# V pages asked for by ScalarE in place of GpSimd, and VectorE's order rearranged, in a decoder layer

## The reference, cut to what matters

```
q, k, v, b, c, xv = split(rmsnorm(x) @ w_in)            # 1024 -> 3072
attn = stick-breaking attention, 8 heads of 64
conv = b * causal_conv3(c * xv)
h = x + concat(rmsnorm(attn), rmsnorm(conv)) @ w_out
h = h + cross_attention(rmsnorm(h), memory K/V)          # 4 heads, 256 memory tokens
h = h + swiglu(rmsnorm(h))
y = rmsnorm(h)
```

## Time and profile before

| | us |
|---|---|
| median of 3 runs | 1208.37 (1198.38 to 1223.24) |
| profiled execution | 1211.09, span 1209.3 |
| PE busy | 1072.4 (89%) |
| VectorE busy | 665.9 (55%) |
| ScalarE busy | 321.4 (27%) |
| GpSimd busy | 409.9 (34%) |

### The profile page before, as it was taken

One profiled execution on the slowest core, in us unless ns is written; L12 is line 12 of the kernel. 1 busy time (PEld: TensorE's weight loads), 2 busy tenths in 40 slices (PEclk: granted clock), 3 DMA queues, 4 the chain that ended last, 5 costly groups with the idle time before them and its releaser, 6 DMA issues.

```text
span 1209.3 us, 28991 instructions
## 1 busy us (share of the span) xinstructions
PE 1072.4 (89%) x11527; PEld 917.1 (76%) x11527; DVE 665.9 (55%) x909; ACT 321.4 (27%) x486; POOL 409.9 (34%) x341
## 2 busy tenths in 40 slices
PE   6889999996678867888599888899999999999997
PEld 3677887774445445556499858899999999999996
DVE  2745647677477676654379356755553002554544
ACT  3412121231233523333422153411211112112121
POOL 0524544442232233444332103343433333433330
PEclk9999999998888889889799999899999999999999
DMA  9888878779898787884652033223221233231222
GB/s 350 316 243 281 284 261 301 244 275 325 326 324 315 284 277 269 276 302 157 222 209 70 16 124 104 73 70 104 69 81 58 79 95 104 69 101 47 66 65 79
DMA packets 126501, 221.16 MB, mean 183 GB/s; under 512 B 9951, under 2 KB 68580, under 8 KB 126388
## 3 DMA queue, kind: packets, MB, share of 16 engines
q1 hardware_dynamic: 103234, 146.63, 36.5%
q0 software_dynamic: 20480, 67.13, 15.5%
q10 hardware_dynamic: 2674, 5.87, 1.3%
HBM read 213.78 MB, written 5.80 MB: 182 GB/s over the span
## 4 chain that ended last, share of the span: by engine, by line
PE 71%; DVE 11%; issue 6%; DMA 6%; SPq 3%; ACT 2%; POOL 1%; DVEq 0%; ACTq 0%; POOLq 0%
PE ps L519 37%; PE ps L1658 11%; PE ps L1761 9%; PE ps L1812 3%; DMA mw_raw<-in_w_in 2%; DMA k_set<-in_cache_sb_k 2%; PE ps L580 2%; DVE k_set L1335 2%; SPq L614 2%; DVE r_sq L693 1%; DVE r_sum L698 1%; SPq L615 1%; PE ps L363 1%; DVE h_lo L424 1%; PE ps L1715 1%
## 5 line engine op out<-in xcount | busy, mean ns | idle before, releaser
L475 POOL TENSOR_TENSOR w_lo<-w_raw,w_hi 128x2048 fp32r<-128x2048 f32 (+3 forms) x49 | 192.8, 3937 | 400.9 <-ACT w_hi L452 363.6
L1761 PE MATMUL ps<-k_set,q_blk 32*32 32x256 f32 x4096 | 142.0, 422 | 62.6 <-issue 47.6
L519 PE MATMUL ps<-h_hi,w_hi 128*128 128x288 f32 x832 | 180.5, 299 | 8.7 <-DVE h_lo L424 5.7
L519 PE MATMUL ps<-h_lo,w_hi 128*128 128x288 f32 x832 | 179.5, 298 | 0.0
L519 PE MATMUL ps<-h_hi,w_lo 128*128 128x288 f32 x832 | 179.4, 297 | 0.0
L1335 DVE STREAM_TRANSPOSE k_set<-k_set 128x1024 f32<-128x1024 f32 x128 | 150.1, 1219 | 37.4 <-DMA k_set<-in_cache_sb_k 36.1
L1761 PEld LDWEIGHTS ps<-k_set,q_blk 32*32 32x32 f32 x4096 | 82.5, 115 | 105.1 <-issue 68.7
L452 ACT ACTIVATE w_hi<-w_raw 128x2048 fp32r<-128x2048 f32 (+3 forms) x47 | 77.9, 1660 | 258.1 <-PE ps L519 228.5
L519 PEld LDWEIGHTS ps<-h_hi,w_hi 128*128 128x128 f32 x832 | 135.6, 191 | 9.8 <-issue 7.2
L964 POOL TENSOR_TENSOR mw_lo<-mw_raw,mw_hi 128x1024 fp32r<-128x1024 f32 x32 | 80.1, 2502 | 177.9 <-ACT mw_hi L1034 177.8
L615 POOL DMA_DIRECT2D v_late<-in_cache_sb_v x160 | 86.2, 539 | 159.4 <-issue 89.7
(11 more groups left out here) (263 smaller groups left out, 1698.9 us busy)
## 6 DMA issues: line engine op xcount, KB each, us to landing
k_set<-in_cache_sb_k SPq DMA_DIRECT2D x256, 256.0 KB, 4.7
v_late<-in_cache_sb_v POOLq DMA_DIRECT2D x160, 256.0 KB, 5.4
v_early<-in_cache_sb_v POOLq DMA_DIRECT2D x96, 256.0 KB, 5.4
mw_raw<-in_w_in SPq DMA_DIRECT2D x12, 1024.0 KB, 10.1
w_raw<-in_w_gate SPq DMA_DIRECT2D x11, 1024.0 KB, 5.4
w_raw<-in_w_up SPq DMA_DIRECT2D x11, 1024.0 KB, 5.3
w_raw<-in_w_down SPq DMA_DIRECT2D x8, 768.0 KB, 4.3
w_raw<-in_w_down SPq DMA_DIRECT2D x8, 640.0 KB, 4.0
```

The source lines that it names most:

```text
L475: return nc.gpsimd.tensor_tensor(w_lo[s][:, ks, :], w_raw[s][:, ks, :], w_hi[s][:, ks, :].bitcast(F32), ALU.subtract)
L519: op = nc.tensor.matmul(ps[:, 2 * t + hf, 0:b - a], weights[s][:, k, t * P:(t + 1) * P], x[:, k0 + k, a:b], start=begin and k == ks[0] and ...
L1761: op = nc.tensor.matmul(tiled(ps[c:c + 32, a, 0:2 * P], 32), blk[r, n:n + 32], k_set[s][r, :, d:d + 32], start=e == 0 and j == 0, stop=e = ...
```

## The change

VectorE: in page chunks all four transposes of the next K half stand together, behind `prompt_weights` and `queries` and around the tile's evacuation, and ahead of `page_weights`. Before, two stood first in the chunk and two behind `page_weights`. `conv_norm` moves from chunk 11 to chunk 10. In the opening `k_blocks(0)` is no longer split around `evac(1)`, and `evac(2)` stands before `page_weights(0)`.

PE: tile 2 stands before the half scores of half 1, and tile 3 before those of half 2.

ScalarE: asks for all V pages. Eight stand in the opening ahead of the memory's squares, four behind the split of tile 2; then from chunk 1 on four at a chunk's start and four behind its weight splits, ahead of `page_sigmoids`. The last eight pages go to `k_set[1]`, which no K half needs any more then, so they wait for the last half scores and no longer for the ring. GpSimd keeps the low parts only.

```diff
         def v_place(n):
+            if n >= 8 * (CHUNKS - 1):
+                m = n - 8 * (CHUNKS - 1)
+                return k_set[1][:, m:m + 1, :], s_v_last[m // 4], 64
...
-        def v_pages(pool, pages):
+        def v_pages(act, pages):
             for n in pages:
-                if n >= RING:
-                    pool.wait_ge(s_vsum, n - RING + 1)
+                if n >= 8 * (CHUNKS - 1):
+                    act.wait_ge(m_["half"], CHUNKS)
+                elif n >= RING:
+                    act.wait_ge(s_vsum, n - RING + 1)
...
             tile_lo(1)
-            pool.wait_ge(s_qkv, 1)
-            pool.wait_ge(s_ev[0], U_X[-1] // 2 + 1)
-            pool.wait_ge(s_ev[1], (U_X[-1] + 1) // 2)
-            pool.wait_ge(s_sq["inb"], 5)
-            v_pages(pool, range(RING))
             tile_lo(2)
...
-                v_pages(pool, range(8 * C + RING, min(8 * C + RING + 4, 8 * CHUNKS)))
                 if 2 * C + 5 < TILES:
                     tile_lo(2 * C + 5)
-                v_pages(pool, range(8 * C + RING + 4, min(8 * C + RING + 8, 8 * CHUNKS)))
...
             def group(g, last):
                 for c in range(8):
                     C, u = 8 * g + c, 8 * g + c - LAST
-                    if 2 * C + 3 < TILES:
+                    if 0 < C < CHUNKS - 1:
+                        v_pages(act, range(8 * C + RING - 8, 8 * C + RING - 4))
+                    if C and 2 * C + 3 < TILES:
                         tile_hi(2 * C + 3)
...
                     if C + 1 in MEM_TILES:
                         tile_hi(MEM_TILES[C + 1])
+                    if 0 < C < CHUNKS - 1:
+                        v_pages(act, range(8 * C + RING - 4, 8 * C + RING if C < CHUNKS - 2 else 8 * CHUNKS))
                     if c % 2 and C + 1 < CHUNKS:
                         page_sigmoids(C // 2 + 1)
...
+            act.wait_ge(s_ev[1], (U_X[-1] + 1) // 2)
+            v_pages(act, range(8))
             act.wait_ge(s_m, 16)
             for m in range(MT):
...
             tile_hi(2)
+            v_pages(act, range(8, RING))
             act.wait_ge(s_bc, 4)
             new_sigmoids(0)
...
+            copy_new_weights(0)
+            tile_hi(3)
             page_sigmoids(0)
-            copy_new_weights(0)
...
                 if C == LAST - 2:
+                    conv_norm()
                     k_blocks(C + 3, range(4))
...
                 add_sums(C - 1)
-                if C == LAST - 1:
-                    conv_norm()
-                if more and C >= LAST:
-                    k_blocks(C + 3, range(2))
                 if c == 0:
                     sample_rows(g)
                 if 1 <= u < 17:
                     prompt_weights(u - 1)
                 if c == 5 and g < GROUPS - 1:
                     queries(g + 1)
+                if more:
+                    k_blocks(C + 3, range(2))
                 if C in MEM_TILES:
                     evac(MEM_TILES[C])
+                if more:
+                    k_blocks(C + 3, range(2, 4))
...
                     step(dve, nc.vector.memset(q_blk[1][:, :], 0.0))
-                    k_blocks(C + 3, range(2))
                 if c == 6 and g < GROUPS - 1:
                     new_weights(g + 1)
-                if more:
-                    k_blocks(C + 3, range(2, 4))
```

More of the change, by code:

```diff
@@ L267, in hybrid_layer @@
         s_v = [sem(f"v_pages{i}") for i in range(RING // 2)]
+        s_v_last = [sem(f"v_last_pages{i}") for i in range(2)]
         s_kt, s_vsum = sem("k_blocks_transposed"), sem("v_page_summed")
@@ L1431, in tile_chunk @@
                     sample_rows(g)
-                evac(2 * C + 2)
+                if C:
+                    evac(2 * C + 2)
                 if C in (2, 4):
@@ L1527, in _ @@
             queries(0)
-            k_blocks(0, range(2))
+            k_blocks(0, range(4))
             evac(1)
-            k_blocks(0, range(2, 4))
             dve.wait_ge(s_sq["ck"], 3)
@@ L1537, in _ @@
             new_weights(0)
+            evac(2)
             page_weights(0)
@@ L1833, in tile_chunk @@
                     new_weight_transposes(g)
-                tile(2 * C + 2)
+                if C:
+                    tile(2 * C + 2)
                 if c == 0 and g:
@@ L1839, in tile_chunk @@
                     pe.wait_ge(s_rt["conv"], 1)
+                if C == 0:
+                    tile(3)
                 half_scores(C + 2, 0)
@@ L1844, in tile_chunk @@
                 sums(C, (0, 1))
-                tile(2 * C + 3)
+                if C:
+                    tile(2 * C + 3)
                 if c == 6:
@@ L1910, in _ @@
             memory_rms()
+            tile(2)
             half_scores(1, 0)
+            new_weight_transposes(0)
             half_scores(1, 1)
-            new_weight_transposes(0)
             pe.wait_ge(s_rt["ck"], 1)
```

6 lines of the change are left out of this document (3 added, 3 removed).

## The result

The changed kernel takes 1220.40 us (median of 4 runs, 1219.32 to 1221.59), the kernel before 1211.39 beside it: a ratio of 1.0094, 95% interval 1.0049 to 1.0140. The forecast was 1196, inside 1160 to 1230. The profiled execution has a span of 1219.7 us against 1209.3. In the table further down, the median and the ratio of the kernel with shared K requests leave out one execution of 1718 us, whose granted clock was 0.56.

A forecast was written before the change was run, and what follows sets the result against it. Gains could come only from PE's 80 us idle in the page chunks, mainly gaps before half scores, or the opening. Terms -40 + 16 + 2 + 8 + 0 + 1 = -13 us gave 1196 us against the median; range 1160 to 1230.

The forecast's parts named there:

- VectorE's late order: Page chunks: transposes ahead of scan and product let half scores start sooner; -40 us in all.
- Slow starts: Page chunks: half scores run slower after long gaps; shorter gaps win back 8 us, half of 15.4.
- V pages on ScalarE: Page chunks: ScalarE's own chain and later V pages cost 13 us, chunk 29 another 3; +16 us together.
- chunk 29: Page chunks: the sum of rows stands behind the page weights and the sigmoids come 3.3 us later; +3 us.
- The surcharge: Two sequencers asking for transfers at once: up to 0.33 us per meeting page, 5 us a pair; forecast did not adopt it.
- Opening: Before the tile chunks: eight page requests and the earlier tile 2 delay sigmoids and tile 6; +8 us, ends 0 and 12.
- Tile chunks: Odd tile chunks: requests delay sigmoids up to 3.1 us each, weights landing earlier repay most; +2 us, 12 kept for the range.
- Last V pages: End of the page chunks: the last eight pages are asked for no earlier; 0 us, ends -6 and +3.
- The rest: Moving conv_norm delays the next chunk's evacuation, and GpSimd's freed time is worth nothing; +1 us.
- the gap only changes its name: Rival, page chunks: K pages land no earlier and VectorE waits for them instead of scanning; 1208 us, chance 0.10.
- ScalarE becomes the bound: Rival, page chunks: at 1.33 us a page ScalarE sets the pair's time, deciding from 1.18; 1249 us, chance 0.16.
- the gaps close fully: Rival, page chunks: pages cost ScalarE well below 1.03 us or overlap activations, so sigmoids come in time; 1166 us, chance 0.30.

The follow-up runs named there:

- shared K requests: Kernel before with only VectorE's new order, plus ScalarE asking for four of each half's eight K pages in later page chunks: 1179.3 us, ratio 0.9761.
- the last pages early in the late order: Kernel before with VectorE's new order and the last eight V pages put in k_set[1], asked for by GpSimd after the last half scores: 1187.0 us.
- the late order alone: Kernel before with only VectorE's new order in the page chunks, V pages staying with GpSimd: 1186.7 us, ratio 0.9806; repeated, 1188.1 us.
- the V pages alone: Kernel before with only the V page requests moved to ScalarE, VectorE's order and the opening as before: 1253.3 us, ratio 1.0385.
- Fixed numbers: Changed kernel with V page numbers fixed in the program, so no register loads on ScalarE and other pages read: 1185.3 us, ratio 0.9811.

## Why the prediction was wrong, step by step

*VectorE's late order, -40 us: this step failed.* Alone it gave 19.3 us in the stretch it acts on; over the four executions that have it with GpSimd's V pages and the K pages as before (282.0, 275.7, 276.3, 279.0) the mean is 23.0. Slow starts (8.3 of 8 forecast) and q_new (6.1 of 5) came as said, and "issue" fell by 23.0 of 27, though here no request stood ahead of the sigmoids, which had been my reason to stop at 27. What failed is to count this as time gained, with no term for what TensorE would wait for next. First K pages: the transposes now come where the pages have not landed, and 28.6 us of the half scores' waits stand behind them, one of 13.2 us among these, where before none did. I had the 36.1 us of VectorE's waits for K pages in hand, named them as a bound, and gave them no term. Second, the sentence that the transposes may delay the page weights by 2.4 us at no cost, because PE has other work first: the tile in that other work waits for the sum of rows, behind scan and product, and the sums wait for evacuations; that took 12.7 us back.

In the changed kernel itself the gaps before the half scores closed as far as forecast. TensorE's waits there ("issue", K set and sigmoids) went from 57.2 to 18.2 us, and the half scores from 92.4 to 85.7. But its idle time in the stretch fell only by 9.5 us, since V pages (15.9 us more) and VectorE's and ScalarE's other products ended other waits, and its busy time did not fall (230.5 to 231.6): the sums behind those waits took 40.3 us in place of 36.7.

*V pages on ScalarE, +16: the size came out, in part by luck.* It was 13.9 us with the order of the change. But the 16 held only ScalarE's own chain, the later V pages and chunk 29; what the requests take by standing ahead of the sigmoids was inside the -40, as gaps left open. By that reckoning the order without the requests had to give more than 40, and it gave 19 to 26. The price of 1.03 us a page, taken as 8.26/8, came as 7.87/8 = 0.98, and the gap that the sigmoids end was 2.2 us. The surcharge that the Trainium skill's locked descriptor hardware would bring (Perfetto Trace Analysis, DMA Instruction — HWDGE (DVE, Sync)) does not show: 115 of ScalarE's 256 requests ran beside one of SyncE's and took 0.355 us (median), the other 141 took 0.349. Sharing K requests between these two queues did not lose, either.

*Opening, +8: +12.3.* Direction and mechanism right, size off. 6.0 are the order itself, 1.8 the requests, 4.5 their meeting in the sigmoids of chunk 1. In my working tile 2 took 6.6 us; it took 9.32, at a granted clock of 0.50 up to 67.9 us and 1.00 from there, behind 3.3 us in which PE stood idle. The first sigmoids came 5.3 us later than forecast, the weights' request (89.00 before) at 102.6 and not at 96.6, and tile 6 6.4 us later; 2.0 us of each is the later start of tile 0. The chain of waits:

```profile
58.38 1.06 ACT mw_hi L1033
59.51 2.37 POOL mw_lo L970
61.92 9.32 PE ps L1664 x48
77.50 3.81 issue
```

*Tile chunks, +2: +6.5.* The 12 kept for the range held it. I let earlier weights repay the requests; the move of four requests behind the sigmoids gave 3.4 of it back, so they do not repay it.

*Last V pages, 0: right*, as the last pages early in the late order show. *The rest, +1*: -2.0; both are less than repeats differ by.

The sum by stretches was +8, +2, -24 and +1; it came as +12.3, +6.5, -8.4 and -2.0. Of the 21 us between, 16 lie in the page chunks. Of the rivals, "the gap only changes its name", which I gave 0.10, was nearest in mechanism: in the late order alone its K pages, in the changed kernel V pages more than K pages, on which VectorE waits 18.3 us there. "ScalarE becomes the bound" names 1249, and the V pages alone gave 1253; that is chance, since its condition of 1.18 us a page was not met. Fixed numbers meet the condition of "the gaps close fully" (0.54 us a page), and gave 1185.3, not 1166.

## What to carry to other kernels

An engine in order pays for every request it issues, 1 us a page here with the page's number read from memory; four requests a chunk cost 16 us in 1220 ahead of the step that others wait for, against behind it. Measure a bundle part by part: one part here was worth -2%, and the bundle hid it. When a reordering closes a gap, work out what stands next in the same engine's program (here the sums of rows and the evacuations) and what feeds the moved step (here K pages, where the DMA engines are full), and give both a term of the sum, not a mention.

## What the runs showed of the hardware

- A register load of a page number costs the engine about as much as the request (0.56 and 0.49 us): eight pages 7.87 us with loads between, 3.88 us for the requests alone when the loads came first, 4.29 with none. A request with a fixed page number took longer by itself, 0.443 us (median) against 0.349 on ScalarE and 0.432 against 0.333 on SyncE.
- The granted clock rose with shorter gaps, in the page stretch from 0.88 before to 0.91 with the late order, 0.94 with shared K requests, and fell to 0.83 with V pages on ScalarE alone. The half scores took 448 ns a matmul before and 415 with the late order.
- A 256 KB page landed in 12.2 us (median) where two 1 MB stores stood in its queue and all 16 DMA engines were busy, and in 8.5 with the stores in another queue.
- In the late order the DMA engines moved 403 GB/s over 25 us at a busy share of 1.04, and K pages asked for around there (300 to 335 us) landed in 14.5 us (median), against 8.4 before, at 327 GB/s.
